# Making sums of weight blocks by adding transfers in main memory, for 26 Strassen slabs in the last projection

## The chip, the cores and the metric

The kernel runs on one core of one Trainium2 chip. The metric is the device time of one execution in microseconds, of which three were taken of the kernel before. Five engines run side by side, each through its own program in order, and meet at semaphores: TensorE (PE in the profile), VectorE (DVE), ScalarE (ACT), GpSimd (POOL) and SyncE (SP), which here only issues transfers.

## What is computed

One decoder layer on 256 tokens of width 2048, in float32:

```python
proj = x @ w_in                                   # 2048 -> 3 x 1024 + 288 + 3 x 1024
mix  = concat(rwkv7(proj), diff_attention(proj)) @ w_out
x    = layer_norm(ALPHA * x + mix) * ln1_gain + ln1_bias
h    = square(relu(x @ w_ff1)) @ w_ff2            # 2048 -> 8192 -> 2048
x    = layer_norm(ALPHA * x + h) * ln2_gain + ln2_bias
```

The change concerns the last product, `h @ w_ff2`: 256 x 8192 times 8192 x 2048.

## The kernel before

Every float32 product is made of three products in the rounded type that TensorE takes at full rate. A matrix is split into a high part (`whi`, the rounded copy, made by ScalarE) and a low part (`wlo` = the matrix minus `whi`, made by VectorE), and hi x hi, lo x hi and hi x lo are added up. So each slab of weights costs one ScalarE copy and one VectorE subtraction beside its matmuls.

Weights come in slabs of 128 partitions x 2048 (1 MB) through four stage buffers (`stage`, NST = 4). SyncE issues the load of slab g when the low part of slab g - 4 is done (`slab`, L439 on: `sp.wait_ge(s_lo, n - (NST - 1))`). `whi` and `wlo` have two buffers each (NHL = 2), so ScalarE starts on slab g when TensorE is through with slab g - 2 (`s_used`).

The stages in order of time: the input projection with the RWKV and attention work woven in (to about 430 us), the output projection (to about 535), the first feed-forward projection FF1 (64 slabs, `pairs`), then the last projection FF2 (64 slabs, `rows` and `quad`). FF2 goes in two sweeps of 32 slabs; a sweep covers one half of the 2048 output columns. A slab holds two blocks of 128 rows of `w_ff2` by two quarters of 512 columns, that is four blocks of 128 x 512. With the two tiles of 128 tokens (a = 0, 1) it is a 2 x 2 times 2 x 2 product of blocks. A plain slab (`rows`) makes it with 8 block products, 24 matmuls of 128x512. A Strassen slab (`quad`, n in `QUAD`) makes it with 7 block products in Winograd's form, 21 matmuls; it needs sums of weight blocks (`tsum`, four of them) and of hidden blocks (`asum`, four of them), and adds into four shared banks of PSUM, which VectorE combines at the end of each sweep (`shared_taken`).

Who does what for a Strassen slab n, in the order in which each engine's program has it:

- VectorE, at slab n - 2: `quad_sums` (L2236 on), three additions of `stage` blocks into `tsum`.
- GpSimd: three subtractions of blocks of `hid` into `asum` (L2388 on), after the `aslo` of the Strassen slab before.
- ScalarE, at slab n - 1: `quad_sums_hi` (L1655 on), `thi` (the rounded `tsum`) and `ashi`.
- VectorE, at slab n: `quad_sums_lo` (L2252 on), `tlo` and `aslo`, which together raise `s_ql` by 2; then `slo` (`split`) and the three-block `wlo` (`lo_own`).
- ScalarE, at slab n: `shi` (`split`) and the three-block `whi` (`hi_own`).
- TensorE (`quad`, L1198 on) waits for `shi`, `slo` and `whi`, makes two products that need no sums, waits for `s_ql`, makes the products with sums, and waits for `wlo` ahead of its last ones.

GpSimd has little to do: four rounds of element-wise work in the input projection (L2354 on), five subtractions `acts` in the first LayerNorm (`x1_lo`, L2373) for which the first slabs of FF1 wait, eight pairs of products and sums with `ln1_gain` and `ln1_bias` (`gained`, L2375 on), then `asum`, and two products with `gain2` (L2402) near the end. It issues no transfer.

Of the kernel before, what the change touches and what calls it, by code (L numbers as in the profile page):

```python
# [16 lines left out]
P = 128  # L17
D = 2048
# [35 lines left out]
QUADS = (tuple(range(4, 29, 3)), tuple(range(38, 60, 3)))  # L54
QUAD = QUADS[0] + QUADS[1]

# [53 lines left out]
def build(nc, t):  # L110

    ctx = ExitStack()
    with ctx:
# [9 lines left out]
        def sem(name):  # L123
# [92 lines left out]
        tsum = at("tsum", 12, [P, 4, 512])  # L216
# [27 lines left out]

        ps = ctx.enter_context(nc.psum_tensor("ps", [P, 8, 512], F32))
# [9 lines left out]
            sem("consts_loaded"), sem("positions_loaded"), sem("attention_consts_loaded"),  # L255
# [4 lines left out]
        s_vec, s_lup = sem("zeros_then_vectors_ready"), sem("lora_weights_loaded")  # L260
# [53 lines left out]
        s_qs, s_qh, s_ql = sem("quad_sums"), sem("quad_sums_rounded"), sem("quad_sums_remainders")  # L314
# [123 lines left out]
        def _(sp):  # L438
# [27 lines left out]
            sp.dma_start(wup[:, :], t["w_up"]).then_inc(s_lup, 16)  # L466
            sp.dma_start(aup[64:128, :], t["a_up"]).then_inc(s_lup, 16)
# [49 lines left out]
            slabs(G_FF2, 0, 2, t["w_ff2"])  # L517
            sp.wait_ge(s_used, G_FF2)
            sp.dma_start(gain2[:, :], t["ln2_gain"].partition_broadcast(P)).then_inc(s_ln2c, 16)
            sp.dma_start(bias2[:, :], t["ln2_bias"].partition_broadcast(P)).then_inc(s_ln2c, 16)  # L520
            slabs(G_FF2, 2, DFF // P // 4, t["w_ff2"])
# [7 lines left out]
        def _(pe):  # L529
# [90 lines left out]
            pe.wait_ge(s_cst, 16)  # L620
            pe.wait_ge(s_lup, 32)
# [576 lines left out]
            def quad(n):  # L1198
# [13 lines left out]
                def lows(acc, x, y, stop):  # L1212
# [3 lines left out]
                own = ((shared[0], plain[0, 0], whole[1], 0), (direct[0, 0], plain[0, 1], whole[2], None))  # L1216
                mixed = ((direct[1, 0], plain[1, 1], added[3], None), (shared[1], summed[1], added[0], 1),
                         (shared[2], summed[0], added[1], 2), (shared[3], summed[2], added[2], 3),
                         (direct[0, 1], summed[3], whole[3], None))
# [61 lines left out]
        def _(act):  # L1281
# [373 lines left out]
            def quad_sums_hi(n):  # L1655

                k = quad_no(n)
                if k:
                    act.wait_ge(s_used, G_FF2 + QUAD[k - 1] + 1)
                act.wait_ge(s_qs, 3 * k + 3)  # L1660
                A(thi[:, :, :], tsum[:, :, :], ACT.Copy).then_inc(s_qh, 1)
                act.wait_ge(s_pl, 2 * NB + 3 * k + 3)
                A(ashi[:, :, :], asum[:, :, :], ACT.Copy).then_inc(s_qh, 1)

            def shared_copied(h):

                act.wait_ge(s_used, G_FF2 + QUADS[h][-1] + 1)
                act.wait_ge(s_ql, 2 * quads_to(h))
                A(tsum[:, 0, :], ps[:, shared_bank(h, 0), :], ACT.Copy).then_inc(s_qh, 1)
# [30 lines left out]
        def _(dve):  # L1700
# [535 lines left out]
            def quad_sums(n):  # L2236

                g, k = G_FF2 + n, quad_no(n)
                src = stage[g % NST][:, :].rearrange("p (j q) -> p j q", j=4)
                if k == 0:  # L2240
                    dve.wait_ge(s_ff, N_FF1)
                    dve.wait_ge(s_lnp, 8)
                else:
                    dve.wait_ge(s_ql, 2 * k)
                dve.wait_ge(s_stage[g % NST], 16 * (g // NST + 1))
                TTn(tsum[:, 0:2, :], src[:, 1::2, :], src[:, 0:1, :].broadcast_to([P, 2, 512]), ALU.add).then_inc(s_qs, 1)
                dve.wait_ge(s_qs, 3 * k + 1)
                TTn(tsum[:, 2, :], tsum[:, 0, :], src[:, 3, :], ALU.add).then_inc(s_qs, 1)
                dve.wait_ge(s_qs, 3 * k + 2)
                TTn(tsum[:, 3, :], tsum[:, 2, :], src[:, 2, :], ALU.add).then_inc(s_qs, 1)  # L2250

            def quad_sums_lo(n):  # L2252
# [5 lines left out]
                TTn(tlo[:, :, :], tsum[:, :, :], f(thi[:, :, :]), ALU.subtract).then_inc(s_ql, 1)  # L2258
# [3 lines left out]
            def shared_taken(h, part):  # L2262

                top, right, bottom, corner = (xres[:, a, quarter(2 * h + q)] for a, q in ((0, 0), (0, 1), (1, 0), (1, 1)))
                copied, v, z = (tsum[:, i, :] for i in range(3))
# [21 lines left out]
            for n in range(1, LAST_PAIR + 2):  # L2287
                g, after = G_FF2 + n, n - QUADS[sweep(n)][-1]
                if n in QUAD:
                    quad_sums_lo(n)  # L2290
                if n <= LAST_PAIR:
                    split(pair_of_hidden(n), n, n % 2, g - 1)
                if n in QUAD:
                    lo_own(g)
# [7 lines left out]
                if n + 2 in QUAD:  # L2302
                    quad_sums(n + 2)
# [48 lines left out]
        def _(pool):  # L2352
# [14 lines left out]

            for a in range(TT_):
# [38 lines left out]
def layout(inputs):  # L2407
# [31 lines left out]
    def sweeps(w):  # L2439

        out = w.reshape(-1, 2, P, 2, D // 2).transpose(3, 0, 2, 1, 4).reshape(-1, P, D).copy()
        for n in QUAD:
            out[n] = out[n].reshape(P, 4, 512)[:, [1, 0, 2, 3], :].reshape(P, D)
# [33 lines left out]
```

## Time and profile before

| | |
|---|---|
| median of 3 runs | 1240.4 us (1239.34 to 1243.26) |
| profiled execution | 1239.0 us, of it span 1237.2 us |
| TensorE | busy 1219.4 us (99%), granted clock 0.997 |
| TensorE weight loads | 1033.4 us (84%), beside the matmuls |
| VectorE | 860.7 us (70%) |
| ScalarE | 619.4 us (50%) |
| GpSimd | 137.7 us (11%) |
| transfers | 222.38 MB, mean 180 GB/s, all issued by SyncE but for instructions |

A share of busy time is a mean over the whole span. Which engine sets the end in a stage is read from the chain of work that ended last and from what each engine waited for.

### The profile page before, as it was taken

The page shows a single profiled execution, that of the slowest core. Times are in us where ns is not written, and L with a number is a line of the kernel's source. Part 1 is how long each engine was busy: PE and PEld are TensorE (multiplying, and loading weights), DVE is VectorE, ACT ScalarE, POOL GpSimd, SP SyncE. Part 2 cuts the span into 40 slices and gives each one's busy share as a digit, 9 for nine tenths or more (in the row PEclk, how much of TensorE's full clock was granted, in tenths as well). Part 3 has the DMA queues.
Part 4 walks back from the last instruction along what each step waited for, and adds up shares of the span by engine and source line. Part 5 has one row for each costly group of instructions (what it writes and reads, how often), then busy time and mean ns, then how long its engine had stood idle before and what let it go on. Part 6 is the DMA issues. An engine that isn't in the chain of part 4 may idle for free.

```text
span 1237.2 us, 22985 instructions
## 1 busy us (share of the span) xinstructions
PE 1219.4 (99%) x9585; PEld 1033.4 (84%) x9585; DVE 860.7 (70%) x909; ACT 619.4 (50%) x674; POOL 137.7 (11%) x94
## 2 busy tenths in 40 slices
PE   8999999999999999999999999999999999999997
PEld 8888888888779878888888888888888888888884
DVE  5688888475766375765554545555689998889987
ACT  5754455546566254453334343434455555565552
POOL 0022112000000000055000000000122221022220
PEclk9999999999999999999999999999999999999998
DMA  9454465332431156635555554545565555555541
GB/s 338 146 213 173 171 246 198 104 138 104 157 117 54 39 222 225 261 105 202 179 194 185 188 193 180 201 174 201 173 269 204 204 204 205 174 206 203 202 168 69
DMA packets 34206, 222.38 MB, mean 180 GB/s; under 512 B 4717, under 2 KB 5101, under 8 KB 8782
## 3 DMA queue, kind: packets, MB, share of 16 engines
q1 hardware_dynamic: 34126, 221.21, 50.0%
q8 instruction: 62, 1.02, 0.3%
q14 instruction: 18, 0.15, 0.0%
HBM read 219.10 MB, written 2.10 MB: 179 GB/s over the span
## 4 chain that ended last, share of the span: by engine, by line
PE 55%; DVE 1%; ACT 0%; issue 0%; DVEq 0%
PE ps L531 55%; DVE stats L2135 0%; DVE xres L2132 0%; DVE xres L2325 0%; DVE xres L2323 0%; DVE xres L2313 0%; ACT xres L1283 0%; DVE xres L2317 0%; DVE moments L2138 0%; PE ps L1175 0%; DVE moments L2145 0%; ACT moments L1283 0%; DVE shift_diag L2339 0%; DVE moments L2144 0%; DVEq L2125 0%
## 5 line engine op out<-in xcount | busy, mean ns | idle before, releaser
L1708 DVE TENSOR_TENSOR wlo<-stage,whi 128x2048 fp32r<-128x2048 f32 x166 | 387.0, 2331 | 244.5 <-ACT whi L1283 243.7
L531 PE MATMUL ps<-acts,whi 128*128 128x512 f32 (+1 forms) x1728 | 535.0, 392 | 3.2 <-DVE wlo L1735 1.9
L1283 ACT ACTIVATE whi<-stage 128x2048 fp32r<-128x2048 f32 (+2 forms) x196 | 361.8, 1847 | 303.0 <-PE ps L531 297.4
L531 PEld LDWEIGHTS ps<-acts,wlo 128*128 128x128 f32 x1680 | 316.1, 188 | 72.1
L531 PE MATMUL ps<-acts,wlo 128*128 128x256 f32 x1680 | 334.9, 278 | 0.0
L531 PEld LDWEIGHTS ps<-acts,whi 128*128 128x128 f32 x1728 | 264.4, 189 | 7.7 <-DVE wlo L1735 2.1
L531 PE MATMUL ps<-whi,shi 128*128 128x512 f32 x402 | 110.8, 389 | 0.0
L531 PE MATMUL ps<-wlo,shi 128*128 128x512 f32 x402 | 110.8, 389 | 0.0
L531 PE MATMUL ps<-whi,slo 128*128 128x512 f32 x402 | 110.8, 389 | 0.0
L1283 ACT ACTIVATE shi<-hid 128x512 fp32r<-128x512 f32 x64 | 40.5, 633 | 127.9 <-PE ps L531 127.9
L531 PEld LDWEIGHTS ps<-wlo,shi 128*128 128x128 f32 x402 | 75.5, 188 | 15.7
L531 PEld LDWEIGHTS ps<-whi,slo 128*128 128x128 f32 x402 | 75.5, 188 | 15.6
L531 PEld LDWEIGHTS ps<-whi,shi 128*128 128x128 f32 x402 | 75.4, 188 | 15.5
L2393 POOL TENSOR_TENSOR asum<-hid 128x256 f32<-128x256 f32 x17 | 20.7, 1219 | 542.7 <-DVE hid L2215 311.8
L531 PE MATMUL ps<-whi,acts 128*128 128x512 f32 (+1 forms) x192 | 53.3, 365 | 1.8 <-POOL acts L2373 0.9
L2097 DVE TENSOR_TENSOR slo<-hid,shi 128x512 fp32r<-128x512 f32 x64 | 46.6, 728 | 11.3 <-ACT shi L1283 11.3
L531 PE MATMUL ps<-whi,oshi 128*128 128x512 f32 x128 | 51.0, 398 | 1.1 <-ACT yf L1283 0.9
L531 PE MATMUL ps<-wlo,oshi 128*128 128x512 f32 x128 | 50.0, 390 | 0.0
L531 PE MATMUL ps<-whi,oslo 128*128 128x512 f32 x128 | 49.9, 390 | 0.0
L2373 POOL TENSOR_TENSOR acts<-x1f,acts 128x512 fp32r<-128x512 f32 x5 | 6.4, 1287 | 335.9 <-ACT acts L1283 335.9
L531 PEld LDWEIGHTS ps<-whi,acts 128*128 128x128 f32 x192 | 32.8, 189 | 9.6 <-issue 5.6
L1283 ACT ACTIVATE TM_TT<-ps 128x512 f32<-128x512 f32 x36 | 19.8, 596 | 41.9 <-PE ps L531 41.9
(290 smaller groups left out, 1394.5 us busy)
## 6 DMA issues: line engine op xcount, KB each, us to landing
stage<-w_ff SPq DMA_DIRECT2D x128, 1024.0 KB, 4.8
stage<-w_in SPq DMA_DIRECT2D x48, 1024.0 KB, 4.9
stage<-w_out SPq DMA_DIRECT2D x16, 1024.0 KB, 4.8
stage<-w_in SPq DMA_DIRECT2D x6, 512.0 KB, 9.4
xstage<-xT SPq DMA_DIRECT2D x4, 512.0 KB, 7.5
TM_TT<-eyes SPq DMA_DIRECT2D x4, 512.0 KB, 7.5
xres<-x SPq DMA_DIRECT2D x1, 2048.0 KB, 9.4
gain<-ln_gain SPq DMA_DIRECT2D x2, 1024.0 KB, 7.7
```

The lines of the kernel that those rows point to most:

```text
L531: return pe.matmul(out, lhsT, rhs, start=start, stop=stop, skip_group_check=True)
L1283: return act.activation(out, in_, func, **kw)
L1708: TTn(wlo[k0 % NHL][:, :], stage[k0 % NST][:, :], f(whi[k0 % NHL][:, :]), ALU.subtract).then_inc(s_lo, 1)
L2097: TTn(slo[h][:, :, :], src, f(shi[h][:, :, :]), ALU.subtract).then_inc(s_alo, 1)
L2373: PT(actlo[:, ks, tok(a)], x1f[:, ks, tok(a)], f(acthi[:, ks, tok(a)]), ALU.subtract).then_inc(s_x1l, 1)
L2393: PT(asum[:, 0:2, :], x[:, 1:2, :].broadcast_to([P, 2, P]), x[:, 0::3, :], ALU.subtract).then_inc(s_pl, 1)
```

## The change

The four sums of weight blocks of each Strassen slab are no longer made by VectorE from the stage buffer. GpSimd makes them in main memory, in a new tensor `made`, by transfers that copy and transfers that add on arrival, two slabs to a batch, 13 batches: seven right after its work in the input projection and six after the first LayerNorm. SyncE loads the sums of each Strassen slab (1 MB) into one of two `tsums` buffers ahead of the slab's own load. `QUADS` names 26 slabs in place of 17: every second one of 2 to 28 and of 37 to 59, where it was every third of 4 to 28 and of 38 to 59. ScalarE's `quad_sums_hi` moves behind `shi` of the slab itself, and VectorE's `quad_sums_lo` behind its `slo`. The loads of `gain2` and `bias2` move from the start of FF2 to behind the last slab. Blocks 2 and 3 of a Strassen slab change places in `w_ff2` as it is laid out, and the LoRA weights and constants share one semaphore.

```diff
-QUADS = (tuple(range(4, 29, 3)), tuple(range(38, 60, 3)))
+QUADS = (tuple(range(2, 29, 2)), tuple(range(37, 60, 2)))
 QUAD = QUADS[0] + QUADS[1]
+SUM_BATCH, SUMS_EARLY = 2, 7
...
-        tsum = at("tsum", 12, [P, 4, 512])
+        tsums = [at("tsum0", 12, [P, 4, 512]), at("tsum1", 9, [P, 4, 512])]
...
+        made = nc.dram_tensor("block_sums", (len(QUAD), P, 4, 512), F32, kind="Internal").ap()
...
-            slabs(G_FF2, 0, 2, t["w_ff2"])
-            sp.wait_ge(s_used, G_FF2)
+            def block_sums(k):
+
+                if k == 0:
+                    sp.wait_ge(s_lnp, 8)
+                elif k == 1:
+                    sp.wait_ge(s_used, G_FF2)
+                else:
+                    sp.wait_ge(s_ql, 2 * k - 2)
+                if k == quads_to(0) + quads_to(0) % 2:
+                    sp.wait_ge(s_pd, 8)
+                if k:
+                    sp.wait_ge(s_sums, 16 * k)
+                sp.wait_ge(s_made, 96 * (k // SUM_BATCH + 1))
+                sp.dma_start(tsums[k % 2][:, :, :], made[k]).then_inc(s_sums, 16)
+
+            for n in range(DFF // P):
+                if n in QUAD:
+                    block_sums(quad_no(n))
+                slab(G_FF2 + n, G_FF2 + n, t["w_ff2"][n])
+            sp.wait_ge(s_ql, 2 * len(QUAD))
             sp.dma_start(gain2[:, :], t["ln2_gain"].partition_broadcast(P)).then_inc(s_ln2c, 16)
             sp.dma_start(bias2[:, :], t["ln2_bias"].partition_broadcast(P)).then_inc(s_ln2c, 16)
-            slabs(G_FF2, 2, DFF // P // 4, t["w_ff2"])
...
                 if n in QUAD:
                     split(hid[:, 2 * m:2 * m + 2, :], g, None, n % 2)
+                    if n - 2 in QUAD:
+                        quad_sums_hi(n)
                     hi_own(g)
...
-                if n + 1 in QUAD:
+                if n + 1 in QUAD and n - 1 not in QUAD:
                     quad_sums_hi(n + 1)
...
-                if n in QUAD:
+                if n in QUAD and n - 2 not in QUAD:
                     quad_sums_lo(n)
                 if n <= LAST_PAIR:
                     split(pair_of_hidden(n), n, n % 2, g - 1)
                 if n in QUAD:
+                    if n - 2 in QUAD:
+                        quad_sums_lo(n)
                     lo_own(g)
...
-                if n + 2 in QUAD:
-                    quad_sums(n + 2)
...
+            def sums_made(batch):
+
+                k0, done = SUM_BATCH * batch, 96 * batch
+                step = QUAD[k0 + 1] - QUAD[k0]
+                w = t["w_ff2"][QUAD[k0]:QUAD[k0] + step * SUM_BATCH:step].rearrange("n p (j q) -> p n j q", j=4)
+                to = made[k0:k0 + SUM_BATCH].rearrange("n p j q -> p n j q")
+                if batch:
+                    pool.wait_ge(s_made, done)
+                pool.dma_start(to[:, :, 0:2, :], w[:, :, 1:3, :]).then_inc(s_made, 16)
+                pool.dma_start(to[:, :, 2:4, :], w[:, :, 2:4, :]).then_inc(s_made, 16)
+                pool.wait_ge(s_made, done + 32)
+                for j in range(2):
+                    pool.dma_start(to[:, :, j, :], w[:, :, 0, :], accum_op=ALU.add).then_inc(s_made, 16)
+                pool.wait_ge(s_made, done + 64)
+                pool.dma_start(to[:, :, 2, :], to[:, :, 0, :], accum_op=ALU.add).then_inc(s_made, 16)
+                pool.wait_ge(s_made, done + 80)
+                pool.dma_start(to[:, :, 3, :], to[:, :, 2, :], accum_op=ALU.add).then_inc(s_made, 16)
+
+            for batch in range(SUMS_EARLY):
+                sums_made(batch)
+
             for a in range(TT_):
                 for G in range(1, 4 - a):
...
+            for batch in range(SUMS_EARLY, len(QUAD) // SUM_BATCH):
+                sums_made(batch)
             pool.wait_ge(s_ff, N_FF1)
```

## Rows read from the trace of the kernel before

**Rows 1.** Chain that ended last: start us, us, engine, tile, line, count

```profile
547.69 667.03 PE ps L531 x3391
```

**Rows 2.** 885 to 1210: busy us by engine (x instructions), clock, DMA share, GB/s

```profile
885.00:1210.00 325.00, 325.00 (x1435) 269.24 (x1434) 287.09 (x234) 188.29 (x162) 64.70 (x53) 1.00 0.56 201
```

**Rows 3.** TensorE's waits, whole span: us in total, times, longest

```profile
PE ps L531 <- POOL acts L2373: 0.9, 3, 0.4
...
PE ps L531 <- ACT yf L1283: 0.9, 1, 0.9
```

**Rows 4.** Timeline of TensorE: start us, us, engine, line, operation, tiles, count

```profile
906.50 0.62 PE L531 MATMUL ps<-whi,shi 128*128 128x512 f32 x2
...
911.26 1.07 PE L531 MATMUL ps<-whi,shi 128*128 128x512 f32 x4
...
916.70 1.07 PE L531 MATMUL ps<-whi,shi 128*128 128x512 f32 x4
```

**Rows 5.** Groups by line, 885 to 1215: busy us, mean ns, idle before

```profile
L2246 DVE TENSOR_TENSOR tsum<-stage 128x1024 f32<-128x1024 f32 x17 | 21.8, 1283 | 0.0
...
L2248 DVE TENSOR_TENSOR tsum<-tsum,stage 128x512 f32<-128x512 f32 x17 | 11.8, 692 | 0.6
```

**Rows 6.** Timeline of ScalarE and VectorE around one Strassen slab

```profile
914.14 1.92 ACT L1283 ACTIVATE thi<-tsum 128x2048 fp32r<-128x2048 f32 x1 [0.24 <-DVE tsum L2250]
...
915.97 0.61 ACT L1283 ACTIVATE ashi<-asum 128x512 fp32r<-128x512 f32 x1
...
916.90 0.63 ACT L1283 ACTIVATE shi<-hid 128x512 fp32r<-128x512 f32 x1 [0.32 <-PE ps L531]
...
917.44 1.48 ACT L1283 ACTIVATE whi<-stage 128x1536 fp32r<-128x1536 f32 x1
...
916.77 2.28 DVE L2258 TENSOR_TENSOR tlo<-tsum,thi 128x2048 fp32r<-128x2048 f32 x1
...
918.97 0.68 DVE L2260 TENSOR_TENSOR aslo<-asum,ashi 128x512 fp32r<-128x512 f32 x1
...
920.18 2.29 DVE L2229 TENSOR_TENSOR wlo<-stage,whi 128x1536 fp32r<-128x1536 f32 x1
```

**Rows 7.** Timeline of GpSimd; in brackets its idle time before

```profile
523.23 1.29 POOL L2373 TENSOR_TENSOR acts<-x1f,acts 128x512 fp32r<-128x512 f32 x1 [330.23 <-ACT acts L1283]
...
887.06 1.12 POOL L2393 TENSOR_TENSOR asum<-hid 128x256 f32<-128x256 f32 x1 [311.77 <-DVE hid L2215]
...
890.72 0.46 POOL L2397 TENSOR_TENSOR asum<-hid,asum 128x128 f32<-128x128 f32 x1
```

**Rows 8.** Transfers: count, KB, us to landing; GB/s in 40 slices of 193:523

```profile
stage<-w_ff SPq DMA_DIRECT2D x128, 1024.0 KB, 4.8
...
xres<-x SPq DMA_DIRECT2D x1, 2048.0 KB, 9.4
...
bias<-ln_bias SPq DMA_DIRECT2D x2, 1024.0 KB, 10.2
...
gup<-g_up SPq DMA_DIRECT2D x1, 512.0 KB, 3.8
...
GB/s 150 181 270 131 55 85 122 130 174 106 108 129 131 129 128 127 199 186 129 127 128 2 2 4 116 84 4 5 123 393 356 8 127 185 199 204 334 316 417 131
```

**Rows 9.** Timeline of the end: VectorE, TensorE, GpSimd

```profile
1180.34 5.06 POOL L2402 TENSOR_TENSOR xres<-xres,gain 128x512 f32<-128x512 f32 x2
...
1194.06 1.75 DVE L2229 TENSOR_TENSOR wlo<-stage,whi 128x1536 fp32r<-128x1536 f32 x1
...
1209.90 2.29 DVE L2297 TENSOR_TENSOR wlo_end<-stage,whi_end 128x2048 fp32r<-128x2048 f32 x1
...
1213.18 0.39 PE L531 MATMUL ps<-whi_end,shi 128*128 128x512 f32 x1
```

**Rows 10.** Timeline of ScalarE at 431 us; in brackets its idle time before

```profile
431.36 1.06 ACT L1283 ACTIVATE gtailr<-gtail 96x1024 fp32r<-96x1024 f32 x1 [18.97 <-DMA gup<-g_up]
```

**Rows 11.** VectorE's copies of `AT`: ns min/median/max, first and last start

```profile
L1884 DVE COPY AF<-AT x8: 220/220/1237, 191.6 to 260.7; 64x128 f32<-64x128 f32 x8
```

More of the change, by code:

```diff
@@ L254, in build @@
         s_cst, s_pos, s_attc, s_levc, s_gup = (
-            sem("consts_loaded"), sem("positions_loaded"), sem("attention_consts_loaded"),
+            sem("consts_and_lora_weights_loaded"), sem("positions_loaded"), sem("attention_consts_loaded"),
             sem("level_masks_loaded"), sem("gate_up_loaded"))
@@ L259, in build @@
         s_vecl, s_lncol = sem("vectors_loaded"), sem("ln1_columns_loaded")
-        s_vec, s_lup = sem("zeros_then_vectors_ready"), sem("lora_weights_loaded")
+        s_vec, s_made = sem("zeros_then_vectors_ready"), sem("block_sums_made")
         s_lora, s_z, s_sig = sem("lora_activated"), sem("decay_logits"), sem("decay_sigmoid")
@@ L313, in build @@
         s_x1a = sem("x1_scaled_act")
-        s_qs, s_qh, s_ql = sem("quad_sums"), sem("quad_sums_rounded"), sem("quad_sums_remainders")
+        s_sums, s_qh, s_ql = sem("block_sums_loaded"), sem("quad_sums_rounded"), sem("quad_sums_remainders")
         s_pd = sem("shared_products_taken")
@@ L465, in _ @@
             slab_half(2, 1)
-            sp.dma_start(wup[:, :], t["w_up"]).then_inc(s_lup, 16)
-            sp.dma_start(aup[64:128, :], t["a_up"]).then_inc(s_lup, 16)
+            sp.dma_start(wup[:, :], t["w_up"]).then_inc(s_cst, 16)
+            sp.dma_start(aup[64:128, :], t["a_up"]).then_inc(s_cst, 16)
             sp.dma_start(cst[:, :], t["consts"][:, 0:C_SMALL]).then_inc(s_cst, 16)
@@ L618, in _ @@
             second_chunk()
-            pe.wait_ge(s_cst, 16)
-            pe.wait_ge(s_lup, 32)
+            pe.wait_ge(s_cst, 48)
             pe.wait_ge(s_lora, 1)
@@ L1215, in quad @@
                 pe.wait_ge(s_hi, g + 1)
-                own = ((shared[0], plain[0, 0], whole[1], 0), (direct[0, 0], plain[0, 1], whole[2], None))
+                own = ((shared[0], plain[0, 0], whole[1], 0), (direct[0, 0], plain[0, 1], whole[3], None))
                 mixed = ((direct[1, 0], plain[1, 1], added[3], None), (shared[1], summed[1], added[0], 1),
                          (shared[2], summed[0], added[1], 2), (shared[3], summed[2], added[2], 3),
-                         (direct[0, 1], summed[3], whole[3], None))
+                         (direct[0, 1], summed[3], whole[2], None))
                 for part in range(2):
@@ L1659, in quad_sums_hi @@
                     act.wait_ge(s_used, G_FF2 + QUAD[k - 1] + 1)
-                act.wait_ge(s_qs, 3 * k + 3)
-                A(thi[:, :, :], tsum[:, :, :], ACT.Copy).then_inc(s_qh, 1)
+                act.wait_ge(s_sums, 16 * k + 16)
+                A(thi[:, :, :], tsums[k % 2][:, :, :], ACT.Copy).then_inc(s_qh, 1)
                 act.wait_ge(s_pl, 2 * NB + 3 * k + 3)
@@ L1668, in shared_copied @@
                 act.wait_ge(s_ql, 2 * quads_to(h))
-                A(tsum[:, 0, :], ps[:, shared_bank(h, 0), :], ACT.Copy).then_inc(s_qh, 1)
+                A(tsums[0][:, 0, :], ps[:, shared_bank(h, 0), :], ACT.Copy).then_inc(s_qh, 1)
             for n in range(1, LAST_PAIR + 2):
@@ L2234, in pair_of_hidden @@
                 return hid[:, 2 * m:2 * m + 2, :]
[L2236 to L2250, printed above, removed]
             def quad_sums_lo(n):
@@ L2257, in quad_sums_lo @@
                 dve.wait_ge(s_qh, rounded_count(n, 1))
-                TTn(tlo[:, :, :], tsum[:, :, :], f(thi[:, :, :]), ALU.subtract).then_inc(s_ql, 1)
+                TTn(tlo[:, :, :], tsums[k % 2][:, :, :], f(thi[:, :, :]), ALU.subtract).then_inc(s_ql, 1)
                 dve.wait_ge(s_qh, rounded_count(n, 2))
@@ L2264, in shared_taken @@
                 top, right, bottom, corner = (xres[:, a, quarter(2 * h + q)] for a, q in ((0, 0), (0, 1), (1, 0), (1, 1)))
-                copied, v, z = (tsum[:, i, :] for i in range(3))
+                copied, v, z = (tsums[0][:, i, :] for i in range(3))
                 p1, p5, p7, p6 = (ps[:, shared_bank(h, i), :] for i in range(4))
@@ L2442, in sweeps @@
         for n in QUAD:
-            out[n] = out[n].reshape(P, 4, 512)[:, [1, 0, 2, 3], :].reshape(P, D)
+            out[n] = out[n].reshape(P, 4, 512)[:, [1, 0, 3, 2], :].reshape(P, D)
         return out
```

## The prediction

> **What bounds the kernel now.** I read the chain of work that ended last first: one unbroken piece of 3391 TensorE matmuls from 547.69 to 1214.72 us, then a short LayerNorm chain [rows 1]. Busy time over the last projection says the same: TensorE 325.00 of 325 us, VectorE 287.09, ScalarE 188.29 [rows 2]. TensorE's waits are all small; the ones that matter here are 0.9 us for ScalarE's `yf` and 0.9 us for GpSimd's `acts` [rows 3]. So time falls only if TensorE gets fewer matmuls, and as long as nobody is late for it.
>
> **What one slab costs.** A Strassen slab starts at 906.50, the next (plain) at 911.26 and the one after at 916.70 [rows 4]: 4.76 us for 21 matmuls and 5.44 for 24, both 0.2267 us each. TensorE pays its full matmul count and nothing else.
>
> **Part 1, nine more Strassen slabs.** 26 − 17 = 9 slabs lose 3 matmuls: 27 x 0.2267 = **6.1 us** off the path, if every deadline holds.
>
> **Part 2, deadlines where a Strassen slab comes every second slab.** Removed from VectorE: the `tsum` additions, 1.28 + 0.69 + 0.69 us [rows 5], 17 times, 45.3 us. Added: 9 x (2.28 `tlo` + 0.68 `aslo`) = 26.6 us, and on ScalarE 9 x (1.92 + 0.61) = 22.8, less what a `whi` of three blocks saves against one of four [rows 6]. Per pair of slabs TensorE now takes 45 x 0.2267 = 10.20 us; VectorE has 2.28 + 0.68 + 2.29 (own `wlo`) + 2.28 (plain `wlo`, the shape of `tlo`) + 2 x 0.68 (`slo`, the shape of `aslo`) = 8.9. It fits on average, so the order within the pair decides. Let B be the start of the plain slab before Strassen slab n; the preceding Strassen slab is then done and its buffers free. ScalarE starts `shi` at B + 0.20 (916.70 to 916.90), next instruction 0.54 later, `thi` at + 0.74, ends + 2.66; `ashi` follows `thi` by 1.83, at + 2.57; the own `whi` follows at + 3.2 and ends at + 4.65 [rows 4, 6]. TensorE needs that at + 5.44: 0.8 us to spare. VectorE runs `tlo` from + 2.7, `aslo` 2.20 later, ends + 5.6; TensorE starts Strassen slab n at + 5.44, has four own matmuls (0.9 us), and loads the fifth's weights at about + 6.1: 0.5 us to spare. The own `wlo` ends at + 7.9 (needed + 9.3), then `slo` and `wlo` of plain slab n + 1 end at + 10.9, needed at + 11.8. All hold, the thinnest by 0.5 us, with nothing left over from pair to pair. Cost taken: 0. Were the chain 0.3 us longer, by waits for several semaphores, it would still be 0; 1 us longer it would cost 0.5 us in each of 24 pairs, 12 us.
>
> The first Strassen slab is now n = 2. GpSimd's `asum` starts at 887.06 once the hidden is there and the third ends at 891.2 [rows 7]; `ashi`, `shi`, `slo` in order end near 894, the slab starts near 895.6 (906.50 − 2 x 5.44). 1.5 us to spare, cost 0.
>
> **Part 3, loading the sums.** SyncE now puts a 1 MB load ahead of each Strassen slab: 3 MB in 10.2 us, 308 GB/s. The trace shows slices of 393 and 417 GB/s, and a 1 MB load landing in 4.8 us [rows 8]. In the queue the slab's own load stands behind the wait for `aslo` of the Strassen slab four before, which comes with the `wlo` that frees its stage anyway; both loads are issued some 15 us before use, so even a landing of 10 us is hidden. For sum 1, SyncE waits for the end of the first projection (906.50 − 4 x 5.44 = 884.7), so slab 4's load is 1 us later than now and wanted 18 us on. Cost 0, up to 0.65 us a pair (3.146 MB / 290 − 10.2; 24 pairs, 16 us) if the loads sustained only 290 GB/s.
>
> **Part 4, making the sums.** Nothing in the trace shows an adding transfer, nor one from GpSimd. A batch of two sums is a chain of four links: two copies of 1 MB together, two additions of 512 KB together, one of 512 KB, one of 512 KB. From below: 2 MB load 9.4 us, 1 MB 4.8, 512 KB 3.8 twice [rows 8], 21.8 us. If an addition moves its bytes twice (it reads what it adds to): 9.4 + 9.4 + 4.8 + 4.8 = 28.4. From above, twice that for reading and writing main memory beside the slab loads: 57. I take 30, nearest to the rows with the bytes counted twice. GpSimd is free from 193.0 (523.23 less the 330.23 it stood idle) and wanted at 523.23: 330 us for seven batches, 47 each. After 575.3 (887.06 − 311.77) it has 311.8 us to the sums of hidden blocks, 52 for each of six [rows 7]. At 30 the early ones end at 403 and the late ones at 755; TensorE waits for neither. Traffic: 4 MB written a batch, 28 MB in 210 us on top of slices that mostly show some 130 GB/s there [rows 8]; loads are issued three slabs ahead and no wait for one shows. Cost 0 at 30 us.
>
> The Trainium skill (DMA: Bandwidth & Descriptors, "Anatomy of one DMA — SWDGE (gpsimd) path") gives a GpSimd transfer about 2.0 us plus its bytes at 436 GB/s. By that a batch of 4.2 MB in four links is 8 + 9.6 = 18 us, an estimate below even my lower end, and the early batches would end near 320; the sum would be the same. No row here shows it.
>
> **Part 5, the end.** `gain2` and `bias2` move from the start of the projection to behind slab 63, which is issued when the own `wlo` of slab 59 ends, at 1195.8 now [rows 9]. `bias` loads take 10.2 us [rows 8], with 4.8 for slab 63 ahead: they land at 1207 to 1212 on the old time axis. VectorE needs them at 1214.7, where TensorE's piece ends. But GpSimd's two products, 5.06 us at 1180 now, then lie beside `wlo_end` (1209.90 to 1212.19), whose slab TensorE takes up at 1213.18 [rows 9]. VectorE's own `wlo` is 1.75 us alone and 2.29 beside GpSimd [rows 6, 9], 0.54 more. Two such stretches less the 0.4 us there is: 0 to 0.7 us. I take 0.4. The order of blocks in `w_ff2` and the merged wait for the constants change no instruction's length: 0.
>
> **The sum.** 1239.0 (the profiled execution; its span is 1237.2) − 6.1 + 0.4 = 1233.3. The median of the runs is 1.4 higher, so **1234.7 us**.
>
> **Rivals.**
> *Batches too slow (slower).* GpSimd runs in order: `acts` for the first slabs of the next projection stands behind batch seven, and TensorE already waits for GpSimd there [rows 3, 7]. From T = 47 us a batch, each further us costs 7 us; T = 55 gives 1234.7 + 7 x 8 = 1291, T = 49 some 1249. For it: my upper end is 57 and adding transfers are unseen. Against: 28.4 already counts their bytes twice. Chance 0.12.
> *Last projection not supplied (slower or nothing).* Either the loads at 308 GB/s or the 0.5 us to spare fails: 0.1 us a pair takes 2.4 us back, 0.3 us 7.2, so from 0.4 us on it is slower than before by more than can be told (see below). At 0.2 us, 1239.5; at 0.65 us, 1250. For it: VectorE is at 8.9 of 10.2. Against: slices above 390 GB/s. Chance 0.13.
> *A batch in flight when `gup` is loaded (smaller gain).* ScalarE stands 18.97 us until `gup` lands (3.8 us after its issue) at 431.36, and TensorE waits 0.9 us for the `yf` behind it [rows 3, 8, 10]. If the seven last past 427 (T above 33), that landing may double: up to 3.8 us back, 1236 to 1238.5. It decides nothing at T = 30. Chance 0.15.
> *GpSimd's descriptor work and VectorE hold each other.* A VectorE copy of 0.22 us took 1.24 while GpSimd worked [rows 11]. Each transfer issued could cost one such 1 us in the solve stage; few would be on the path: 1235 to 1239. Chance 0.05. The Trainium skill (SBUF — State Buffer, "Who interferes with whom") says that VectorE's two-port modes and GpSimd, descriptor generation included, shut each other out; the copy agrees for ordinary GpSimd instructions.
> *It does not do what it says.* Were the additions served without sharing anything, the time would be the forecast less the tail cost; were GpSimd's first transfer to need some set-up, it adds a few us once. Within the range; chance 0.03.
>
> **How the numbers follow.** Forecast 0.52; the five rivals 0.48. A measurement here can tell about 0.3%, 3.7 us: below 1236.7 is faster. Faster: 0.52, half of the `gup` case (0.08), a little of the rest (0.03): 0.63. Slower (above 1244.1): 0.12 for the batches, 0.06 for supply: 0.18. Same: 0.19. The range runs from 1232.5 (no tail cost, a run at the lower end) to 1246, which leaves out most of the first rival and the worst of the second, about 0.17.
>
> **What would show it.** TensorE's slabs in the last projection still 4.76 and 5.44 us, back to back, 27 matmuls fewer, the span some 6 us shorter; VectorE about 19 us less busy and ScalarE some 20 more. From GpSimd's transfers T is read directly: early batches over near 400, and GpSimd idle before 523. Wrong: a TensorE wait for GpSimd's `acts` longer than 0.9 us (first rival), repeated waits for `aslo`, `tlo` or a load after 895 (second), a longer wait for `yf` near 433 (third). If T is over 47 the forecast falls whatever else holds.

## The result, and the profile after

The changed kernel takes **1276.15 us** (median of six executions, 1269.56 to 1285.01) against 1239.82 for the kernel before: a ratio of 1.0291, 95% interval 1.0239 to 1.0343. It is 36 us slower, where 1234.7 was forecast and 1246 was the upper end of the range. The profiled execution is the slowest of the six, 1285.01 us; its span of 1283.2 is 46.0 more than before's, so what is read from it explains somewhat more than the 36 us of the medians.

**TensorE's waits first**, as for the kernel before [rows 3]: us in total, times, longest.

```profile
PE ps L551 <- issue: 29.6, 16, 4.5
PE ps L551 <- ACT yf L1302: 7.6, 1, 7.6
...
PE ps L551 <- DVE slo L2118: 1.7, 1, 1.7
PE ps L551 <- POOL acts L2399: 1.3, 3, 0.6
```

The wait for GpSimd's `acts`, by which I would have known slow batches, is 1.3 us. New is **"issue", 29.6 us**: TensorE stands still and no semaphore, engine or transfer shows as the cause. In the kernel before it was 1.1 us in all:

```profile
PE ps L531 <- issue: 1.1, 2, 0.9
```

The wait for `yf` went from 0.9 to 7.6.

**Where in time.** The same instructions of GpSimd as in [rows 7], in the changed kernel:

```profile
192.87 0.87 POOL L2381 DMA_DIRECT2D block_sums<-w_ff  x1
...
450.99 0.71 POOL L2381 DMA_DIRECT2D block_sums<-w_ff  x1 [6.39 <-DMA block_sums<-block_sums]
...
490.15 1.13 POOL L2389 DMA_DIRECT2D block_sums<-block_sums  x1 [11.80 <-DMA block_sums<-block_sums]
572.62 1.28 POOL L2399 TENSOR_TENSOR acts<-x1f,acts 128x512 fp32r<-128x512 f32 x1 [81.34 <-ACT acts L1302]
...
936.77 1.12 POOL L2421 TENSOR_TENSOR asum<-hid 128x256 f32<-128x256 f32 x1 [14.99 <-DVE hid L2236]
```

`acts` starts at 572.62 instead of 523.23, 49.4 us late, and `asum` at 936.77 instead of 887.06, 49.7 late. So the whole loss lies ahead of 523, beside the seven early batches; the six late ones cost 0.3 us, and from there to the end of the span 3.7 us of the 49.7 come back. Six of the early batches took 450.99 − 192.87 = 258.1 us, 43.0 each; GpSimd was done at 491.3 and then waited 81.34 us for ScalarE. It held nobody up.

**The solve and the output projection**: busy us of TensorE (x instructions), its weight loads, VectorE, ScalarE, GpSimd, then granted clock, share of the 16 transfer engines, GB/s.

```profile
200.00:300.00 100.00, 90.85 (x1900) 76.54 (x1895) 53.42 (x62) 49.01 (x65) 14.31 (x14) 1.00 0.92 231
320.00:370.00 50.00, 50.00 (x286) 38.90 (x286) 34.93 (x103) 31.89 (x64) 6.01 (x6) 1.00 0.92 240
385.00:490.00 105.00, 78.66 (x1735) 68.12 (x1735) 35.01 (x47) 36.19 (x54) 15.24 (x15) 0.87 0.74 162
640.00:920.00 280.00, 280.00 (x1609) 244.33 (x1608) 147.02 (x101) 108.97 (x76) 32.25 (x32) 1.00 0.96 269
```

The first and the third of these windows in the kernel before (the same times, for the third not quite the same work):

```profile
200.00:300.00 100.00, 100.00 (x2138) 84.78 (x2135) 57.35 (x67) 53.74 (x71) 0.00 (x0) 1.00 0.38 136
385.00:490.00 105.00, 101.49 (x1664) 84.47 (x1662) 58.51 (x66) 47.90 (x53) 0.00 (x0) 1.00 0.39 142
```

Here is the riddle. In two stretches TensorE loses time beside transfer engines 92% and 74% full, and in two it loses nothing beside engines 92% and 96% full. Full engines alone don't stop it. What differs is the instruction count: 1900 matmuls in 100 us and 1735 in 105, against 286 in 50 and 1609 in 280.

**The instruction queue.** The page's list of queues, with packets, MB and share of the 16 engines:

```profile
q1 hardware_dynamic: 37870, 248.48, 52.3%
q0 software_dynamic: 21216, 54.53, 24.0%
q8 instruction: 61, 1.00, 0.3%
```

q8 fetches the engines' instructions, 61 pieces of 16 KB; the page counts its time against the same 16 engines. (The Trainium skill, "Runtime: NRT & Kernel Launch", Terms, has each engine's instruction memory refilled in 16 KiB blocks; 1.00 MB in 61 packets agrees.) Between 205 and 300 us fourteen of them come, one each 7 us, while q0 alone holds 54.8% of the engines; between 600 and 880, in the loops of the next projection, one:

```profile
q0 software_dynamic: 3522, 8.92, 54.8%
...
q8 instruction: 14, 0.23, 1.0%
```

```profile
q0 software_dynamic: 8160, 20.97, 42.0%
q8 instruction: 1, 0.02, 0.0%
```

From 200 to 300 us TensorE has 3795 matmuls and weight loads for its fourteen pieces, some 270 a piece; in straight code the number of instructions sets how often a piece is needed.

The trace has a q8 packet at 410.07, 418.26, 432.28 and 442.90 us. TensorE's waits there end 2.3 to 2.9 us behind each start; three of the four rows (start of the instruction after the wait, in brackets the wait):

```profile
412.40 0.90 PE L551 MATMUL ps<-kttm,TM_TT 64*64 64x64 f32 x12 [4.55 <-issue]
...
420.79 1.73 PE L551 MATMUL ps<-vtm,kbt 64*64 64x64 f32 x51 [2.50 <-issue]
...
434.62 0.58 PE L551 MATMUL ps<-whi,oshi 128*128 128x512 f32 x1 [3.39 <-issue]
```

This holds for nearly all of them. In the traces of all fourteen kernels of this document TensorE has 87 waits marked "issue". 73 end 1.2 to 1.6 us behind the end of a q8 packet; the other 14 are one in each kernel, 0.26 to 0.36 us long, at one place of the program. Of the changed kernel's 29.6 us the first kind makes 29.2. Of TensorE's other waits, 12 to 15 in a kernel, at most two end in that band. And a packet itself takes no longer: its median is 0.96 us in the kernel before, in the changed one and in one without batches (`e1` below).

My reading: TensorE ran out of instructions, since the piece that holds the next ones came late, held up before it moved, by the batches' transfers.

**The clock.** After such waits TensorE runs at 1.2 GHz instead of 2.4 for a while, in five stretches ahead of the last LayerNorm: 3.4 us from 307.5, and 6.8 us each from 409.9, 433.8, 447.5 and 478.2. Not every such wait is followed by one: behind those of 2.25 us (to 240.7) and 2.54 us (to 291.7) the clock stayed at 2.4 GHz. Two rows of the windows:

```profile
410.00:417.00 7.00, 4.59 (x90) 4.59 (x91) 2.34 (x2) 1.19 (x2) 1.40 (x2) 0.52 0.81 202
434.00:440.00 6.00, 5.38 (x72) 4.13 (x72) 0.70 (x2) 0.00 (x0) 1.13 (x1) 0.50 0.40 50
```

**`yf`.** ScalarE waits for `gup` as in [rows 10], but 35.18 us; its landing went from 3.8 to 12.0:

```profile
478.67 1.06 ACT L1302 ACTIVATE gtailr<-gtail 96x1024 fp32r<-96x1024 f32 x1 [35.18 <-DMA gup<-g_up]
```

**The account** of the 49.4 us: "issue" waits 28.5 more, `yf` 6.7 more, 30.6 us at half the clock, of which up to half, 15.3, is lost. Together 50.5; TensorE idles in parts of the slow stretches (4.59 of 7.00 us busy above), so a little is counted twice. This is the account of the slowest execution.

### The profile page after: what moved, and what is told of

It reads as the page before. It is cut to its first block, busy times and chain, and to the rows that moved or that the text cites. A ratio compares the mean times of both kernels' runs of the same rounds, so it can differ in the third digit from the quotient of the medians.

```text
span 1283.2 us, 22839 instructions
## 1 busy us (share of the span) xinstructions
PE 1229.5 (96%) x9558; PEld 1039.6 (81%) x9558; DVE 852.3 (66%) x876; ACT 635.0 (49%) x692; POOL 294.7 (23%) x199
## 3 DMA queue, kind: packets, MB, share of 16 engines
q1 hardware_dynamic: 37870, 248.48, 52.3%
q0 software_dynamic: 21216, 54.53, 24.0%
## 4 chain that ended last, share of the span: by engine, by line
PE 52%; DVE 2%; issue 0%; ACT 0%; DVEq 0%
PE ps L551 52%; DVE wlo L1729 0%; DVE slo L2118 0%; DVE stats L2156 0%; DVE xres L2153 0%; DVE xres L2330 0%; DVE xres L2328 0%; DVE xres L2318 0%; ACT xres L1302 0%; DVE xres L2322 0%; DVE wlo_end L2304 0%; DVE xres L2276 0%; DVE xres L2285 0%; DVE tsum L2277 0%; ACT tsum L1302 0%
## 5 line engine op out<-in xcount | busy, mean ns | idle before, releaser
L551 PE MATMUL ps<-acts,whi 128*128 128x512 f32 (+1 forms) x1728 | 535.9, 393 | 2.3 <-DVE wlo L1729 1.2
L1729 DVE TENSOR_TENSOR wlo<-stage,whi 128x2048 fp32r<-128x2048 f32 x157 | 372.5, 2372 | 239.6 <-ACT whi L1302 238.9
L551 PEld LDWEIGHTS ps<-acts,wlo 128*128 128x128 f32 x1680 | 316.3, 188 | 72.7
L551 PE MATMUL ps<-acts,wlo 128*128 128x256 f32 x1680 | 335.2, 279 | 0.0
L551 PEld LDWEIGHTS ps<-acts,whi 128*128 128x128 f32 x1728 | 264.3, 189 | 6.8 <-issue 2.0
L551 PE MATMUL ps<-whi,shi 128*128 128x512 f32 x348 | 97.2, 389 | 0.0
L551 PE MATMUL ps<-whi,slo 128*128 128x512 f32 x348 | 97.1, 389 | 0.0
L551 PE MATMUL ps<-wlo,shi 128*128 128x512 f32 x348 | 97.1, 389 | 0.0
L2421 POOL TENSOR_TENSOR asum<-hid 128x256 f32<-128x256 f32 x26 | 53.7, 2067 | 171.5 <-DVE aslo L2265 156.5
L2263 DVE TENSOR_TENSOR tlo<-tsum,thi 128x2048 fp32r<-128x2048 f32 x26 | 59.8, 2301 | 27.4 <-ACT thi L1302 27.4
L551 PEld LDWEIGHTS ps<-whi,shi 128*128 128x128 f32 x348 | 65.2, 188 | 13.9 <-issue 0.4
L551 PEld LDWEIGHTS ps<-wlo,shi 128*128 128x128 f32 x348 | 65.3, 188 | 13.6
L551 PEld LDWEIGHTS ps<-whi,slo 128*128 128x128 f32 x348 | 65.3, 188 | 13.5
L2385 POOL DMA_DIRECT2D block_sums<-w_ff x26 | 30.4, 1394 | 161.2 <-DMA block_sums<-w_ff 161.2
L551 PE MATMUL ps<-whi,oshi 128*128 128x512 f32 x128 | 53.0, 414 | 11.3 <-ACT yf L1302 7.6
L2118 DVE TENSOR_TENSOR slo<-hid,shi 128x512 fp32r<-128x512 f32 x64 | 59.1, 924 | 6.4 <-ACT shi L1302 3.5
L2425 POOL TENSOR_TENSOR asum<-hid,asum 128x128 f32<-128x128 f32 x26 | 58.9, 2265 | 2.0
L551 PE MATMUL ps<-whi,acts 128*128 128x512 f32 (+1 forms) x192 | 53.2, 364 | 2.2 <-POOL acts L2399 1.3
L2387 POOL DMA_DIRECT2D block_sums<-block_sums x13 | 14.7, 1128 | 174.3 <-DMA block_sums<-w_ff 174.3
L551 PE MATMUL ps<-whi,oslo 128*128 128x512 f32 x128 | 51.8, 405 | 0.0
```

The costliest lines, as they stand in the source:

```text
L551: return pe.matmul(out, lhsT, rhs, start=start, stop=stop, skip_group_check=True)
L1729: TTn(wlo[k0 % NHL][:, :], stage[k0 % NST][:, :], f(whi[k0 % NHL][:, :]), ALU.subtract).then_inc(s_lo, 1)
L2118: TTn(slo[h][:, :, :], src, f(shi[h][:, :, :]), ALU.subtract).then_inc(s_alo, 1)
L2263: TTn(tlo[:, :, :], tsums[k % 2][:, :, :], f(thi[:, :, :]), ALU.subtract).then_inc(s_ql, 1)
L2385: pool.dma_start(to[:, :, j, :], w[:, :, 0, :], accum_op=ALU.add).then_inc(s_made, 16)
L2387: pool.dma_start(to[:, :, 2, :], to[:, :, 0, :], accum_op=ALU.add).then_inc(s_made, 16)
```

## The experiments

All are edits of the changed kernel and keep its 26 Strassen slabs in the last projection, with a 1 MB load ahead of each. Where sums aren't made, a slab of weights is loaded in their place, so those Strassen slabs compute other numbers with the same instructions. Line numbers shift with the edits: TensorE's L551 is L550 to L588 here.

**Is it the sums or the slabs?** `e1_none_made` loads other blocks of the weights in place of the sums and makes none:

```diff
-                sp.wait_ge(s_made, 96 * (k // SUM_BATCH + 1))
-                sp.dma_start(tsums[k % 2][:, :, :], made[k])
+                sp.dma_start(tsums[k % 2][:, :, :], t["w_ff2"][QUAD[k]].rearrange(...))
...
-            for batch in range(SUMS_EARLY):
-                sums_made(batch)
...
-            for batch in range(SUMS_EARLY, len(QUAD) // SUM_BATCH):
-                sums_made(batch)
```

`e2_late_only` keeps the second of these loops, `e3_early_only` the first, and `e4_early_copies` the first without `accum_op` in its transfers.

> Changed kernel without any of GpSimd's transfers; SyncE loads a weight slab in place of each slab of sums (26 loads of 1 MB at the same places), so the last projection is computed with wrong sums but with the same instructions. Theory (instruction supply): the whole loss comes from GpSimd's transfers in flight while TensorE runs through long straight code, so here 1239.8 - 6.1 + 2.3 (the tail as it showed in the changed kernel) = 1236, no TensorE wait marked issue above 1 us, clock not halved before the end. Rival (the last projection or SyncE's extra loads cost something): above 1240.

> Changed kernel with the six late batches only (575 to about 890 us); the sums of the first 14 Strassen slabs are replaced by weight slabs, so these are computed with wrong sums. Theory (instruction supply): the first projection runs its matmuls in a hardware loop, its instructions need no fetch, and the late batches cost nothing: 1236, as e1. Rival (GpSimd's transfers cost their time wherever TensorE works, 7 us a batch as in the early stretch): 1236 + 6 x 7 = 1278.

> Changed kernel with the seven early batches only; the sums of the last 12 Strassen slabs are replaced by weight slabs. Theory (instruction supply): all of the loss is here, 1270 to 1285. Rival (late batches share in it): below 1265.

> e3 with plain copies in place of the additions on arrival: the same transfers, bytes, places and waits, nothing is added, so the sums are wrong. Theory (instruction supply through shared transfer engines): what matters is that the engines are full, so most of the loss stays, 1260 to 1280, with TensorE waits marked issue. Rival (the read-modify-write of the additions is what hurts): 1236 to 1245.

| | median us | ratio to before (1241.06) | "issue" | `yf` |
|---|---|---|---|---|
| `e1_none_made` | 1236.82 | 0.9969 (0.9957 to 0.9981) | 2.8 | 0.9 |
| `e2_late_only` | 1237.94 | 0.9987 (0.9971 to 1.0003) | 2.8 | 1.6 |
| `e3_early_only` | 1267.38 (2 runs) | 1.0214 (1.0187 to 1.0240) | 15.2 | 6.2 |
| `e4_early_copies` | 1257.7 (2 runs) | 1.0136 (1.0085 to 1.0187) | 19.7 | 1.1 |

Without the sums the 26 slabs are 4.2 us faster than before; the late batches add 1.1, no more than the intervals leave open; the early ones carry the loss, though in these two executions 30 us against `e1`, not the changed kernel's 39. Both `e3` and `e4` came 2 to 3 us below the range expected. Adding isn't needed for the loss: the two executions with copies alone took 1250.53 and 1264.88 us, 14 and 28 more than `e1`. Whether adding makes the kernel slower two executions can't tell (1264.88 against 1265.98 in the profiled ones), but it lengthens a batch. Both moved 29.36 MB through q0, and the adding chain (first row), cut into more packets, took half as much engine time again:

```profile
q0 software_dynamic: 11424, 29.36, 12.8%
```

```profile
q0 software_dynamic: 7840, 29.36, 8.9%
```

The batches of copies took 34.9 us instead of 44.0 and were over some 20 us before `gup` was loaded, which landed in 3.6 us, against 9.2 in `e3`. So the `yf` wait goes with a batch in flight at that load, and the "issue" waits don't.

**Does the place decide?** Two batches only, each time a stretch of its own: `e5_two_at_193` where the changed kernel has them, `e6_two_at_303` in the output projection behind slab 43, `e10_one_at_394` one batch where the densest code runs.

```diff
+            pool.wait_ge(s_lo, 43)          # e6; e5: no wait; e10: s_lo, G_OUT + 1
+            for batch in range(2):          # e10: one
+                sums_made(batch)
```

> Changed kernel with only the first two batches made, from 193 us on (to about 282); all other sums are replaced by weight slabs and are wrong. That stretch holds TensorE's small 64x64 matmuls of the solve, a fetch of instructions every 5 to 6 us. Theory (instruction supply): the changed kernel lost 13 us from 205 to 290, so 1236.8 + about 12 = 1249, with TensorE waits marked issue. Rival (cost goes with the number of batches, 7 us each): 1251. The pair e5/e6 decides.

> The same two batches, same bytes and waits, but started when the low part of slab 42 is done (about 303 us), in the stretch to 386 where TensorE's instructions are large matmuls and a fetch comes every 20 us; the other sums are wrong as in e5. Theory (instruction supply): nothing lost, 1237 to 1239. Rival (bytes or batches count wherever they lie before the first projection, through late weight loads or main memory): as e5, about 1250.

> One batch only, started when the low part of slab 51 is done (about 394 us), where TensorE's code is densest (a fetch every 3.5 us); all other sums are replaced by weight slabs and are wrong. e5's two batches cost 6.3 us against e1, e6's 3.5. Theory (instruction supply): the price of a batch follows how densely instructions are fetched, so this one costs more than a batch of e5: 1236.8 + 6 to 12 = 1243 to 1249, waits marked issue between 395 and 435. Rival (a uniform price of about 3 us a batch): 1240.

`e5`: 1243.08 us, ratio 1.0027 (1.0008 to 1.0046), 7.2 us for two batches by the two ratios (against `e1`), where I had expected 12; "issue" waits of 0.79, 1.41 and 1.78 us and 3.4 us at half the clock. `e6`: 1240.27, 1.0006 (0.9996 to 1.0016), 4.6 us. I had expected 0 to 2; up to 383 TensorE lost nothing, and then, the second batch's last link having been issued at 383.03, it ran into the dense code with waits of 0.75 and 2.58 us and 3.4 at half the clock. `e10`: **1249.31 us**, 1.0077 (1.0048 to 1.0106), 13.4 us for a single batch of 4.2 MB:

```profile
409.28 0.39 PE L555 MATMUL ps<-whi,oshi 128*128 128x512 f32 x1 [2.08 <-issue]
...
422.48 0.37 PE L555 MATMUL ps<-vtm,ktm 64*64 64x64 f32 x2 [6.12 <-issue]
```

A batch thus costs from next to nothing to 13 us by its place. `e10` stands clear of the other two; between `e5` and `e6` the intervals overlap, and only the waits of the one profiled execution each (6.3 and 5.1 us of "issue", 2.8 in `e1`) tell them apart. The fetches fit the places; here are those of `e1`, undisturbed, from 193 to 303, 303 to 386, and 386 to 430 us (and none from 600 to 880):

```profile
q8 instruction: 18, 0.29, 1.0%
```

```profile
q8 instruction: 6, 0.10, 0.5%
```

```profile
q8 instruction: 10, 0.16, 1.5%
```

One each 6, 14 and 4.4 us, in the order of the prices as far as they can be told.

**Is it GpSimd's kind of transfer?** `e11_sync_copies` makes no sums; SyncE copies 24 times 1 MB from main memory to main memory on its own queue, 12 of them singly between its slab loads from 212 to 314 us, four together at 359 and eight together at 398:

```diff
+                    sp.dma_start(made[...].rearrange("n p j q -> n p (j q)"), t["w_ff2"][...]).then_inc(s_made, 16)
```

> No sums are made (sums wrong as in e1). In their place SyncE issues 24 plain copies of 1 MB from w_ff2 to main memory between its slab loads, 12 of them from 209 to 330 us and 12 from 350 to 430. Theory (full transfer engines starve the instruction fetches, whoever fills them): 1242 to 1262, TensorE waits marked issue in both stretches. Rival (GpSimd's own queue or its descriptor making does it): 1237, as e1.

1253.86 us, ratio 1.0108 (1.0079 to 1.0137). No GpSimd transfer runs, and the wait is there; 14.6 us of "issue" in all, and 13.6 us at half the clock:

```profile
PE ps L561 <- issue: 14.6, 8, 5.3
```

13.0 of the 14.6 us lie beside the eight copies, between 390 and 440 us (engines 84% full from 398 to 431), and 1.3 beside the twelve single ones (60% full from 193 to 303, where `e5` had 79%). So TensorE waits for instructions when the engines are full whoever fills them; GpSimd's descriptors aren't needed for it.

**The tail.** `e7_none_made_tail` is `e1` with `gain2` loaded in the middle of the projection, so that GpSimd's first product is done early:

```diff
+                if n == 33:
+                    sp.dma_start(gain2[:, :], t["ln2_gain"].partition_broadcast(P)).then_inc(s_ln2c, 16)
...
-            pool.wait_ge(s_ln2c, 32)
+            pool.wait_ge(s_ln2c, 16)
```

> e1 (no sums made, weight slabs loaded in their place, sums wrong) with gain2 loaded in the middle of the last projection, so that GpSimd's two products with it run before the last slabs, as in the kernel before; bias2 stays last. Theory (my part 5 had the right mechanism and too small a price): TensorE's 1.7 us wait for slo near the end goes, 1236.8 - 1.7 to 2.3 = 1235. Rival (that wait comes from the denser Strassen slabs, not from GpSimd): 1236.8.

1235.24 us, ratio 0.9967 (0.9956 to 0.9978): against `e1`'s 0.9969 no difference that the medians can tell, but the profiled spans are 1232.0 and 1234.1, and the wait of 1.7 us for `slo` is gone. The changed kernel's tail, the same instructions as [rows 9]:

```profile
1251.76 6.56 POOL L2430 TENSOR_TENSOR xres<-xres,gain 128x512 f32<-128x512 f32 x2 [17.43 <-DMA bias<-ln_bias]
...
1253.82 3.38 DVE L2304 TENSOR_TENSOR wlo_end<-stage,whi_end 128x2048 fp32r<-128x2048 f32 x1
1257.13 1.75 DVE L2118 TENSOR_TENSOR slo<-hid,shi 128x512 fp32r<-128x512 f32 x1
```

and in `e7`:

```profile
1205.85 2.29 DVE L2304 TENSOR_TENSOR wlo_end<-stage,whi_end 128x2048 fp32r<-128x2048 f32 x1
1208.05 0.69 DVE L2118 TENSOR_TENSOR slo<-hid,shi 128x512 fp32r<-128x512 f32 x1
```

Beside GpSimd's products the two VectorE instructions take 2.15 us more together. (The Trainium skill, "SBUF — State Buffer", Who interferes with whom, says that a VectorE instruction with two inputs in SBUF contends with a GpSimd instruction that reads it; these rows agree.)

**A version with the batches elsewhere.** If the place decides, all 26 sums should be had at almost no cost. `e8_spread` unrolls GpSimd's loop in the first projection and puts links of the chain between its rounds, from 31.6 us, some more behind slab 43, and seven batches after the LayerNorm, with the last addition of a batch and the first copies of the next issued together. `e9_spread_six_late` leaves six there and takes the seventh link by link between the Strassen sums of the last projection; `e12_spread_last` only moves its last link:

```diff
+            pool.wait_ge(s_lo, 4)
+            advance(4)
+            kk_round(0)
+            advance(2)
...
+            pool.wait_ge(s_lo, 43)
+            advance(6)
...
+            advance(19)                     # e8: 22
...
+                if k in (2, 5, 8, 11):
+                    advance(1)
+                elif k == 14:
+                    advance(3)              # e9: 4
+                elif k == 17:
+                    advance(1)              # e9: none
```

> The whole computation, all 26 slabs with true sums, but the batches placed where TensorE fetches few instructions: three and a half batches from 30 to 185 us between GpSimd's four rounds of element-wise work, one and a half from 303 on, seven after the first LayerNorm, one inside the last projection; the last addition of a batch goes together with the copies of the next; gain2 as in e7. Theory (instruction supply): near e7, 1235 to 1238, faster than before by 0.2 to 0.4%. Rival (the transfers cost several us a batch in any stretch with weight loads, or late batches hold up asum): above 1242.

> e8 with six batches instead of seven between the first LayerNorm and the last projection, and two made inside the last projection (one spread over the first sweep, one in the 50 us between the two sweeps' Strassen slabs); all sums true. e8 lost 20 us because GpSimd came out of its seventh late batch at 915 us while TensorE wanted the sums of hidden blocks at 900, and some 10 us more while the clock was halved over it. Theory (instruction supply): that wait goes, 1236 to 1239, faster than before by 0.1 to 0.3%. Rival (transfers inside the last projection make its loads late, or GpSimd late): above 1241.

> e9 with the last addition of its last batch moved behind the sums of hidden blocks of the eighteenth Strassen slab. In e9 GpSimd waited for three transfers in a row (18.1, 16.7 and 11.8 us) between the two sweeps and came to its next sums at 1089 us, 3.7 us late for TensorE, and the clock was halved for 3.4 us behind it. Theory: both go, 1241.7 - 3.7 - 1.7 = 1236.3, faster than before by 0.2 to 0.4%. Rival (another deadline a little later takes the wait over, or single executions lose their few us elsewhere): 1239 to 1242.

`e8`: 1258.34 us, ratio 1.0144 (1.0124 to 1.0163), but no longer where the changed kernel loses: "issue" is 2.8 in all. Its seventh late batch wasn't over, GpSimd came to `asum` late, and through ScalarE's order TensorE waited for `whi`:

```profile
915.54 1.17 POOL L2453 TENSOR_TENSOR asum<-hid 128x256 f32<-128x256 f32 x1
```

```profile
920.47 0.77 PE L588 MATMUL ps<-whi,shi 128*128 128x512 f32 x1 [19.98 <-ACT whi L1339]
```

This is the first rival of the prediction, at the sums of hidden blocks instead of `acts`, in a kernel in which it applies. Merging the links hardly shortened a batch: the late ones still took 48.6 us, against 50.8. The wait, and 23.9 us at half the clock around it, are why it missed the 1235 to 1238 expected. `e9`: 1241.73, 1.0010 (0.9994 to 1.0025): behind the sums of k = 14 GpSimd waited 18.07, 16.73 and 11.75 us in a row for its own links, and TensorE 3.71 up to 1093.45, as the rival of its expectation has it. `e12`: **1235.43 us**, ratio 0.9962 (0.9950 to 0.9973), faster than both kernels, by 4.7 and by 40.7 us, with the same transfers:

```profile
PE ps L588 <- issue: 2.4, 4, 1.0
PE ps L588 <- ACT yf L1339: 1.1, 1, 1.1
```

```profile
q0 software_dynamic: 21216, 54.53, 23.3%
```

54.53 MB in 21216 packets, as in the changed kernel, 0.6 us below `e7`'s ratio, which has the same tail and no sums: made at these places, the sums cost nothing that can be measured. The first three and a half batches run there from 31.6 us on, beside straight code of large matmuls:

```profile
32.00:185.00 153.00, 152.24 (x929) 132.24 (x928) 122.39 (x133) 86.40 (x106) 47.10 (x33) 1.00 0.94 272
```

The engines are 94% full and TensorE loses nothing (151.79 us busy in `e1`); seven instruction pieces come in these 153 us, one each 22. So straight code is not the trouble by itself either, but how often it needs a piece.

## Why the prediction was wrong

**Part 1 held.** In the changed kernel a Strassen slab starts at 966.06, the plain one at 970.82 and the next at 976.26: 4.76 and 5.44 us, and TensorE has 9558 matmuls instead of 9585. `e7` gets 0.33% of the 0.49% that 6.1 us are; 1.3 us of the rest may be its longer "issue" waits (2.4 against 1.1), which come without any batch, but also just behind instruction pieces.

**Parts 2 and 3 held.** In the changed kernel no wait for `aslo`, `tlo` or a load came up, with spare of 0.5 us forecast at the thinnest (`e7` and `e12` show one of 0.3 us for `aslo`). ScalarE is 15.6 us busier (some 20 forecast). VectorE is 8.4 us less busy, not 19: its instructions grew longer where GpSimd's `asum` now lies beside them (`slo` from a mean of 0.73 to 0.92 us in the last projection, the four-block `wlo` from 2.29 to 2.44), which the spare took up.

**Part 4 is where it failed**, at "Cost 0 at 30 us", and in two ways: the length of a batch, and what its traffic costs. The smaller: T was 43 us early and (879.02 − 624.94) / 5 = 50.8 late, not 30. The bounds, 21.8 to 57, held it, and so did the limits, 47 and 52: `acts` was no later than its own chain, and `asum` had 14.99 us in hand. The links, by the median from issue to landing, were:

```profile
block_sums<-w_ff POOLq DMA_DIRECT2D x26, 1024.0 KB, 10.3
...
block_sums<-w_ff POOLq DMA_DIRECT2D x26, 512.0 KB, 11.6
block_sums<-block_sums POOLq DMA_DIRECT2D x26, 512.0 KB, 8.1
```

Two 512 KB additions together took longer than two 1 MB copies together, and one alone 8.1 us where I had put 4.8; I had taken them at twice a load's bytes. (The figures of the Trainium skill, "DMA: Bandwidth & Descriptors", Anatomy of one DMA — SWDGE (gpsimd) path, gave an estimate of 18 us a batch; the rows have more than twice that.)

The larger is the term "Traffic: 4 MB written a batch, 28 MB in 210 us", put at 0. I asked of it only whether the slabs' loads still come in time, and they do (SyncE's loads of the late stretch land in a median of 7.8 us instead of 4.8, and nobody waits). I didn't ask **who else uses the 16 engines**. In place of 0 the profiled execution shows 28.5 us more of "issue" waits, 6.7 for `yf` and up to 15.3 of halved clock. The instruction queue stands in the page of the kernel before as one line of a fraction of a percent; what matters of it is not its share but when TensorE needs the next piece. No rival had it, and none of their prices could have reached 36 us by their own mechanism at T = 43.

**The rivals.** Slow batches: didn't happen (1.3 us for `acts`), and would have at T above 47, as `e8` shows in another place. The last projection not supplied: no. **A batch in flight at `gup`: it did happen**, from the very condition given (T above 33), but cost 6.7 us, not up to 3.8: the landing tripled, 3.8 to 12.0, rather than doubled. GpSimd's descriptor work against VectorE: I named the solve stage, where part of the loss does lie, but the wrong cause: `e11` has TensorE's waits with none of GpSimd's transfers.

**Part 5**: mechanism right, size off. The wait for `slo` and the delay of `wlo_end` come to 2.15 us of VectorE time, of which TensorE shows 1.7 us as a wait; 0 to 0.7 was forecast. I had counted two stretches of 0.54 us, each from an instruction of 1536 columns; `slo` alone gained 1.06 and `wlo_end` 1.09, and GpSimd's products took 6.56 us instead of 5.06.

**Shown and not shown.** Shown: the loss follows the traffic (`e1`, `e3`), follows its place (`e5`, `e6`, `e10`, `e12`), and doesn't need GpSimd or adding (`e4`, `e11`). Shown in time: 73 of the 87 "issue" waits end 1.2 to 1.6 us behind an instruction piece, and the pieces themselves are no slower than before. Inferred from that: that each is a wait for the piece, and that the piece stood in the queue for an engine. The profile names no releaser for these waits and tells when a fetch moves, not when it was asked for; no run changes the instruction supply alone. Open: why the changed kernel's executions lie between 1269.6 and 1285, and why seven early batches cost some 39 us where `e5`'s pace for two, 3.6 each, and `e10`'s 13.4 for one between them don't add up to it exactly.

## What to carry to other kernels

Before transfers are put "in the background", list everything that uses the transfer engines in that stretch, the instruction queue too, and count its packets window by window: here the loops fetched one piece in 280 us and straight code of large matmuls one in 22 us, and both bore full engines, while unrolled code with thousands of small matmuls is a consumer with a deadline every 4 to 7 us. Place bulk traffic over the former; here that turned 36 us lost into 4.7 gained without a byte less (a few tenths of it by the tail of `e7`). And a wait of a few microseconds on TensorE costs more than itself, since the clock that is granted behind it may be half.

## What the runs showed of the hardware

- Beside transfers that fill the engines, whether GpSimd (`e10`: 6.12 us) or SyncE (`e11`: 5.26) issued them, TensorE has waits with no releaser, which end 1.2 to 1.6 us behind a 16 KB instruction piece; the pieces take 0.3% of the engines' time. The Trainium skill ("SBUF — State Buffer", Who interferes with whom) says that a DMA never contends with a compute engine; of the SBUF's ports no run here shows otherwise, but transfers do hold TensorE up, by the reading above by way of its instructions.
- GpSimd's transfers within main memory are dear in engine time: 54.53 MB of them took 24.0% of it in the changed kernel, where 248.48 MB of loads took 52.3%, about twice as much per byte. With adding, 29.36 MB took 12.8%, without 8.9%. That they stay within main memory is not what makes them so: SyncE's copies in `e11` put 25.16 MB more on q1 in 768 packets and raised its time from 56.8% of 1234.1 us (`e1`) to 60.4% of 1252.2, some 55 us of all 16 engines or 2.2 us a MB, where q1's other traffic has 2.8. Their packets are of 33 KB, those of GpSimd's of 2.6 KB with adding and 3.7 KB without; what part that has, no run separates.
- Issuing the last addition and the next copies together shortened a batch only from 50.8 to 48.6 us (`e8`), where the engines were 96% full already.
- TensorE's clock stood at 1.2 GHz for 3.4 to 10.2 us beside or behind waits of 1.5 to 7.6 us (10.2 with the 6.12 us of `e10`), and for 23.9 us with the 19.98 us of `e8`; but behind some of 2.1 to 2.5 us it stayed at 2.4 GHz. `e1`, whose longest "issue" wait is 1.3 us, shows no drop ahead of the last LayerNorm.
